# A two-layer decoder step: the odd layer's pool latents kept on chip, its recurrence cut in quarters, and query weights requested earlier

## The reference, cut to what matters

```
u, cq, ckv, kpe = split(rms_norm(x) @ w_in)              # 512 + 256 + 128 + 32 columns
# C: diagonal complex state space, 32 groups x 64 states, in and out 512 channels
s_t = abar * s_{t-1} + bbar u_t ;  y = Re(C s) + D u ;  z = gelu(y);  oc = z * sigmoid(z w_glu + b)
# D: latent attention, 8 heads; prompt: causal over 256 tokens
q = (rms_norm(cq) w_uq), split 64 | 32, normed, second part rotated
# sample: per request 8 pages x 128 cached latents c_all (128 wide) and rotary keys k_all (32 wide)
k = rms_norm(c_all w_uk) * g ;  v = c_all w_uv
o = softmax((q_nope . k + q_pe . k_all) / sqrt(96)) v
x = x + concat(oc, o) @ w_out ;  x = x + peer(rms_norm(x))
```

## Time and profile before

| | |
|---|---|
| median of three executions | 2640.33 us |
| the profiled execution: time, span | 2625.28 us, 2623.6 us |
| PE busy | 2120.1 us, 81% of the span |
| DVE busy | 1206.9 us, 46% |
| ACT busy | 630.0 us, 24% |
| POOL busy | 956.5 us, 36% |
| mean DMA rate | 202 GB/s |
| mean granted TensorE clock | 0.89 |

### The profile page before, as it was taken

The page is one execution under the profiler, slowest core; times in us unless marked ns, Lnnn a source line. Parts: engine busy times, 40 slices in busy tenths (PEclk is TensorE's granted clock), DMA queues, the critical chain, the costliest instruction groups (busy, mean ns, idle before and its releaser), DMA issues.

```text
span 2623.6 us, 36788 instructions
## 1 busy us (share of the span) xinstructions
PE 2120.1 (81%) x13673; PEld 1535.1 (59%) x13673; DVE 1206.9 (46%) x3473; ACT 630.0 (24%) x952; POOL 956.5 (36%) x872
## 2 busy tenths in 40 slices
PE   8897799999998666666667875899999997666665
PEld 3553479999996333333443323489999995333232
DVE  2432369813333533674266453289623333333332
ACT  1421114455552000000133330015455550000000
POOL 0001007970003666666012222018850005656664
PEclk9678899999998888888867887899999998888887
DMA  5415324444447999999400033404445448999998
GB/s 209 171 52 193 114 112 145 154 164 165 166 164 244 356 354 339 338 342 356 153 8 27 27 97 123 152 35 168 153 163 167 163 167 293 353 335 356 355 345 297
DMA packets 163476, 529.55 MB, mean 202 GB/s; under 512 B 20930, under 2 KB 35298, under 8 KB 162786
## 3 DMA queue, kind: packets, MB, share of 16 engines
q0 software_dynamic: 89152, 313.05, 33.0%
q1 hardware_dynamic: 74146, 214.14, 23.7%
HBM read 524.42 MB, written 2.69 MB: 201 GB/s over the span
## 4 chain that ended last, share of the span: by engine, by line
PE 58%; DMA 18%; POOL 10%; issue 7%; DVE 4%; ACT 2%; POOLq 1%; SPq 0%; DVEq 0%; ACTq 0%
DMA v_slot<-in_peer_v,v_rows 16%; PE bank L617 15%; PE bank L762 9%; PE bank L764 9%; PE bank L763 9%; PE bank L821 7%; POOL v_slot L562 6%; POOL u_low L551 3%; PE bank L1050 2%; POOLq L376 1%; PE bank L816 1%; PE bank L637 1%; DMA region<-in_cache_a_kt 1%; PE bank L1056 1%; PE bank L721 1%
## 5 line engine op out<-in xcount | busy, mean ns | idle before, releaser
L562 POOL DMA_INDIRECT v_slot<-in_peer_v,v_rows x576 | 546.1, 948 | 767.9 <-PE bank L764 441.1
L762 PE MATMUL bank<-h_parts,u_high 128*128 128x288 f32 x2048 | 606.6, 296 | 5.1 <-POOL u_low L551 4.6
L763 PE MATMUL bank<-h_parts,u_high 128*128 128x288 f32 x2048 | 604.4, 295 | 0.0
L764 PE MATMUL bank<-h_parts,u_low 128*128 128x288 f32 x2048 | 602.8, 294 | 0.0
L821 PE MATMUL bank<-v_slot,weight_columns 128*32 128x512 f32 x2048 | 321.5, 755 | 273.4 <-DMA v_slot<-in_peer_v,v_rows 269.4
L551 POOL TENSOR_TENSOR u_low<-u_slot,u_high 128x1024 fp32r<-128x1024 f32 x120 | 320.2, 2678 | 369.7 <-ACT u_high L1217 369.6
L762 PEld LDWEIGHTS bank<-h_parts,u_high 128*128 128x128 f32 x2048 | 384.1, 188 | 8.3 <-POOL u_low L551 7.7
L764 PEld LDWEIGHTS bank<-h_parts,u_low 128*128 128x128 f32 x2048 | 385.7, 188 | 0.0
L763 PEld LDWEIGHTS bank<-h_parts,u_high 128*128 128x128 f32 x2048 | 384.5, 188 | 0.0
L1217 ACT CAST u_high<-u_slot 128x1024 fp32r<-128x1024 f32 x256 | 268.8, 1050 | 398.1 <-PE bank L764 287.2
L821 PEld LDWEIGHTS bank<-v_slot,weight_columns 128*32 128x32 f32 x2048 | 72.0, 124 | 395.0 <-issue 343.0
(11 more groups left out here) (337 smaller groups left out, 2140.8 us busy)
## 6 DMA issues: line engine op xcount, KB each, us to landing
u_slot<-in_peer_ut SPq DMA_DIRECT2D x256, 512.0 KB, 3.3
w_q<-in_peer_w_q SPq DMA_DIRECT2D x8, 2048.0 KB, 15.8
v_slot<-in_peer_v,v_rows POOLq DMA_INDIRECT x576, 6.2
region<-in_ev_w_in SPq DMA_DIRECT2D x4, 2048.0 KB, 15.7
region<-in_cache_a_kt SPq DMA_DIRECT2D x8, 960.0 KB, 12.1
region<-in_cache_a_v SPq DMA_DIRECT2D x8, 960.0 KB, 14.3
ckv_pages<-in_pool_ckv SPq DMA_DIRECT2D x52, 128.0 KB, 2.1
region<-in_pool_kv POOLq DMA_DIRECT2D x32, 128.0 KB, 3.1
```

What stands on the lines that cost most here:

```text
L562: pool.indirect_dma_start(out=VS[n % NVS], out_offset=None, in_=v_rows, in_offset=bass.IndirectOffsetOnAxis(ap=IDX[:, t:t + 1], axis=0)).t ...
L762: pe.matmul(bank, uh, HR[:, 0, c, :], start=(c == 0), stop=False)
L763: pe.matmul(bank, uh, HR[:, 1, c, :], start=False, stop=False)
L764: ins = pe.matmul(bank, ul, HR[:, 0, c, :], start=False, stop=(c == KC - 1))
```

## The change

- **Latents on chip.** The turned latents of a request's four pages go to a place of their own (`CKPT`, sixteen tiles, and `CKPT_FIRST`, four, for the first pass) and are read twice, by the key norms and by the scores. The values (the other 64 KB of each page) are fetched apart (`CKPV`). Fetching is split between SP (requests 0, 1, 4, 5) and POOL (2, 3, 6, 7). The first pass is loaded by POOL behind the last expert group of layer 0. No refill waits for squares any more.
- **Recurrence by quarters.** Four quarters of four chunks. The sample states are computed once for all sixteen chunks in a tile of their own (`BUS`) rather than twice for eight.
- **First quarter of the key norms, and quarters 0 and 1 of B u, ahead of the prompt attention.** B is turned at the start of the layer, and the sums' weights `SUMW` are set there.
- **New order.** Key norms, states' outputs, sample scores and values are interleaved; the sample attention for r = 0 runs before the recurrence ends, and the gate before the last values.
- **Early query weights.** The first quarter of `w_q` is requested in layer 0 right behind `w_out`, in layer 1 when the gate and the first values are done. In layer 1 the quarters change places (`W_QS`).

Cut to its core, by engine:

```diff
 SP
+    load(W_QS[0][0], peer_w_q[0, :, :, 0:512])          # behind load(W_OUT, ...)
-    wait states_ready 2; stores of states; 24 full pages; wait y_ready 4; 24 full pages;
-    wait pages_used 1; 4 pages; wait pages_used 4, 6: w_out1 halves
+    wait qct_ready 10;     for b in 0,1: 8 latent pages each;  TBLDN
+    for c in 0,1: wait quarter_ready c+1;  for b in 4,5: 4 latent pages each
+    wait y_ready 2;        for b in 0,1: 8 value pages each
+    wait sd_scores 1;      for b in 4,5: 8 kpe pages each;  for b in 4,5: 8 value pages each
+    wait samples_ready, quarter_ready 4: w_out1 halves;  stores of states
+    wait oc_ready 4, pages_used 4:  load(W_QS[1][0], peer_w_q[1, :, :, 0:512])
 POOL
-    wait qk_ready 3: 32 kpe pages;  wait s5_bt_ready: 64 latent pages, refills wait key_squares
-    then 8 full pages, 32 kpe pages, 4 full pages
+    wait v_used (all of layer 0):  for b in 0..3: first 4 latent pages each
+    wait qct_ready 10:  for b in 2,3: 8 latent pages each;  for b in 0..3: 8 kpe pages each
+    for c in 0,1: wait quarter_ready c+1;  for b in 6,7: 4 latent pages each
+    wait sd_scores 1:   for b in 2,3: 8 value pages each;  for b in 6,7: 8 kpe pages each
+    wait y_ready 4:     for b in 6,7: 8 value pages each
 PE  (odd)
+    turn B;  norm;  w_in1;  latents;  q, k, v of the new tokens
+    states_in(0); states_in(1); B u of the sample rows; key_norms(0,0)
     turn q and k; prompt attention; turn its output
+    states_in(2); absorbed queries
+    key_norms(0,1); states_out(0); states_in(3); key_norms(1,0); states_out(1)
+    sample_states_out(); latent_scores(0); key_norms(1,1); latent_turn(0)
+    states_out(2); latent_values(0); states_out(3); latent_out_turn(0)
+    latent_scores(1); [zg_ready] gate product; latent_turn(1); latent_values(1); latent_out_turn(1)
 ACT (odd), from the copies of q, k, v on
+    qk_root(0); states_in(0); qk_root(1); states_in(1); BUS copies
+    key_squares 0..7; qk_root(2); key_squares 8..15; copies of turned q, k; prompt exps; states_in(2)
+    key_squares 16..31; states_in(3); 32..39; key_root(0); 40..55; latent_exp(0); 56..63
+    latent_turn(0); key_root(1); gelu; latent_exp(1); sigmoid; latent_turn(1)
 DVE (odd), from the per-head norms on
+    key_vars(0,0); QG, QPE copies; prompt attention
+    states_turn/scan/turn_back(0); absorbed_queries; turn/scan/turn_back(1)
+    key_vars(0,1); out_of_states(0); sample_states; states_turn(2); key_vars(1,0)
+    out_of_states(1); out_of_sample_states; states_scan(2); key_scales(0); latent_scores(0)
+    states_turn_back(2); states_turn(3); key_vars(1,1); states_scan(3); out_of_states(2)
+    states_turn_back(3); latent_out(0); out_of_states(3); latent_out_turned(0)
+    key_scales(1); latent_scores(1); gate products; latent_out(1); latent_out_turned(1)
```

More of the change, by code:

```diff
@@ new lines, in build @@
+        states.at += 4096
+        STMP = states.take("s5_sample_tmp", 4, SCH, DEC_B)
+        KPEN = states.take("kpe_new", NS, parts=DR)
+        TBLDN = states.take("mask_new", 2, NS)
+        RKN = states.take("key_scale_new", DH, DEC_T)
+        RKNX = states.take("key_scale_new_x", NS)
+        mid = Row(R2_0 + 3264, R2_0 + 15552)
+        kt0 = mid.at
+        Q = mid.take("mla_q", 3, DH, DQK)
+        KCAT = mid.take("mla_k", 2, DH, DQK)
+        KR = mid.take("mla_k_raw", 3, 512)
+        S_SD = tile_at("mla_sample_scores", [PAST + NS], kt0 + 4 * PAGES * P)
@@ L333, in build @@
         BT = end.take("s5_b_t", 2, 4, P)
-        STMP = end.take("s5_sample_tmp", 4, SG2, DEC_B)
+        end.at += 256
         LASTP = end.take("s5_last_prompt", 2, SCH)
@@ L1012, in odd, with states_in @@
                         pe.matmul(bank[0:rows, :], CKT[:, a:a + rows], w, start=True, stop=True).then_inc(a_full, 1)
+                pe.wait_ge(sem("s5_bt_ready"), 2)
+                def states_in(g):
+                    for s in range(4 * g, 4 * g + 4):
+                        rows = slice(32 * (s % 4), 32 * (s % 4) + 32)
+                        for k in range(2):
+                            bank = to_act()
+                            pe.matmul(bank[:, 0:SEQ], BT[rows, k, g, :], UT[rows, g, 0:SEQ], start=True, stop=True).then_inc(a_full, 1)
@@ new lines, in odd @@
+                states_in(0)
+                states_in(1)
+                four = [to_act() for _ in range(4)]
+                for g in range(4):
+                    for k in range(2):
+                        for q in range(4):
+                            rows = slice(32 * q, 32 * q + 32)
+                            ins = pe.matmul(four[q][:, (4 * k + g) * NS:(4 * k + g) * NS + NS], BT[rows, k, g, :], UT[rows, g, SEQ:NT], start=True, stop=True)
+                            if g == 3 and k == 1:
+                                ins.then_inc(a_full, 1)
@@ L1315, in odd, with states_in, qk_root @@
                         act.activation(ST8I[0:rows, m, 0:3], ST8[0:rows, m, 0:3], ACT.Sqrt).then_inc(sem("latent_rinv"), 1)
+                def states_in(g):
+                    for q in range(4):
+                        for k in range(2):
+                            copy_out(BU[g][:, k, q, :], full()[:, 0:SEQ], "bu_ready")
+                def qk_root(t):
+                    rows = TILES[t][1]
+                    act.wait_ge(sem("qk_var"), t + 1)
+                    act.activation(ST8I[0:rows, t, 0:24], ST8[0:rows, t, 0:24], ACT.Sqrt).then_inc(sem("qk_rinv"), 1)
                 for t, rows, a in TILES:
@@ L1370, in odd @@
                         act.nop().then_inc(sem("sd_pt"), 1)
+                key_squares(16)
+                key_squares(24)
+                states_in(3)
+                key_squares(32)
+                key_root(0)
+                key_squares(40)
+                key_squares(48)
+                latent_exp(0)
+                key_squares(56)
+                latent_turn(0)
+                key_root(1)
+                act.wait_ge(sem("y_ready"), 5)
+                for m in range(4):
+                    act.activation(ZG[:, m, :], Y[:, m, :], ACT.Gelu_apprx_tanh).then_inc(sem("zg_ready"), 1)
+                latent_exp(1)
+                for m in range(4):
+                    bank = full()
+                    link(act.activation(SGM[:, m, :], bank[:, 0:NT], ACT.Sigmoid, bias=BGLU[:, m:m + 1]))
+                    act.nop().then_inc(a_free, 1)
+                    act.nop().then_inc(sem("sgm_ready"), 1)
+                latent_turn(1)
                 act.wait_ge(sem("qabs_ready"), 1)
@@ L2013, in odd, with key_scales, out_of_states @@
-                dve.wait_ge(sem("key_roots"), 1)
-                link(dve.reciprocal(RK, RK))
-                for r in range(2):
+                    say("samples_ready")
+                def key_scales(r):
+                    dve.wait_ge(sem("key_roots"), r + 1)
+                    link(dve.reciprocal(RK[:, r, :], RK[:, r, :]))
+                def out_of_states(g):
+                    bank = full()
+                    STT(Y[:, g, 0:SEQ], UT[:, g, 0:SEQ], DSKIP[:, g:g + 1], bank[:, 0:SEQ], ALU.mult, ALU.add)
+                    free()
+                    say("y_ready")
```

498 lines of the change are left out of this document (288 added, 210 removed).

## The result

The changed kernel takes 2570.05 us (median of 4 runs, 2563.28 to 2577.24) beside 2642.72 us for the kernel before (4 runs): a ratio of **0.9729, 95% interval 0.9689 to 0.9769**. The prediction was 2565 us with a range of 2545 to 2600, and faster. Timed once more in a later comparison it gave 0.9716 (0.9679 to 0.9754), 2550.08 beside 2625.13: 72.7 and 75.1 us less, where 75 were forecast.

What follows compares the result with a forecast made beforehand. No engine is full: in the odd mixer's attention and the 251 us behind it, engines take turns, and PE waited 45 us for latent pages. Mixer 65 plus query weights 10 gives 75 us off 2640.3: 2565, range 2545 to 2600.

Steps and rivals of the forecast that it cites:

- The sum: Whole kernel: 65 us less in the odd mixer plus 10 from early query weights, 75 us in all, predicted median 2565.
- the query weights: Before the first query product in both layers: waits of 5.4 and 5.2 us, 0.2 kept each, so 10.2 us go.
- Part 1: Odd mixer, ahead of the prompt attention: work moved there makes the attention end 23.2 us later.
- The third root: First key-norm pass: root of the third tile comes 8 us late, but DVE still ends at 1364, under the pass.
- interference of the first loads: POOL's latents beside `w_in1` and small inputs: between 0 and 3.5 us, 2.5 taken as cost.
- Part 2: Odd mixer, behind the prompt attention: engine-by-engine layout to output projection at 1572.2; 1574.7 with 2.5 us of load interference, against 1639.5.
- The rule of the table loads: ACT in mid-pass: skill's 1.38 us drain per table load would end two passes 1.4 us later, gain 72; rows followed instead.
- 1 (the order catches, 45): Mixer passes and scores each wait 6 to 8 us more than laid out; 30 us go, gain 45, 2595; chance 0.17.
- 2 (better, 92): Attention at full clock saves 4 us, no load interference 2.5, passes closed up 10; gain 92, 2548; chance 0.10.
- 3 (POOL held by DVE): Each of POOL's 104 path loads waits 1.22 us for DVE's product; 45 us slower, 2685; chance 0.04.
- 4: Gains eaten to within 13 us, as by loads arriving late at several passes at once; 2635; chance 0.03.
- The small slacks: Page loads behind the attention: all land just in time, with 0.6 to 4.6 us in hand.

## Why the prediction was right

**The sum.** Forecast 64.8 for the mixer, measured 62.9. Forecast 10.2 for the query weights, measured 4.6 + 6.0, and 10.6 by undoing them. 75.0 against 73.5, and 72.7 and 75.1 by the medians. Agreement to 2 us is partly luck, as steps below are off by up to 2.5 us each, in both directions.

**Part 1.** The first score operation stood 86.3 us behind the first product of `w_in1` (1358.42 in the earlier trace rows; 1272.17) and stands at 113.1, and at 110.3 to 113.1 in the variants that leave this part alone: 24 to 27 us later, where 23.2 and 2.5 of interference were forecast. The pass took 25.3 us, not 24.1, and the sample rows' B u with its copies 5.0, not 3 (1349.27 to 1354.24). The third root was late (DVE waited 11.55 us for it) and hidden, as said. Against these stands the interference of the first loads: the new tokens' values end at 60.8 to 63.2 us of the mixer with the loads in the way and at 61.3 with them later (61.6 before), so it cost up to 1.6 us in the profiled execution and nothing in others, in place of 2.5.

**Part 2.** From the first score operation to the output projection it was 281.1 us; forecast 190.6, measured 191.3. The steps: quarters 20.2 (20.0), passes 25.2 to 26.3 (24.1 to 25.6), sample states 13.0 (11.5), absorbed queries 3.6 (2.0), sample outputs 0.9 (2), quarter output 1.1 (1.2), values 8.8 (10.6), reciprocal 6.55 (6.5). The errors are of both signs and cancel: what DVE's sample states took more, the values gave back. Sixteen of their products now take 1.91 us where the earlier trace rows had 3.62, at a granted clock of 1.00 (1567 to 1572) and behind the gate product; before, PE had just waited 3.92 us for the exponent and the clock was 0.50 (1623 to 1627). The sum had carried the slower price over. The waits came where they were laid out: DVE for the last sums 7.29 (7.2), PE for score banks 10.36 and 3.13. The wait of 45.3 us for pages is gone. It was worth 34.7 us of path by the run that took it out alone, and 26.8 of the mixer in that kernel's own order; the 33 us behind the last sums came with the new order, by the timelines.

**What it did not see.** The sum priced the four parts of the title as one layout and said of the first pass only that it is gone from behind. It never set the 24 us at the head against what DVE would wait without it. The run that moves it back shows them equal. The forecast was right because the layout was right, not because each part pays.

**The rule of the table loads.** ACT's timeline in the last pass, table load, exponent and the next square:

```profile
1516.94 1.28 ACT L1452 ACT_TABLE_LOAD   x1 [0.17 <-ACT key_squared L1427]
1518.23 1.18 ACT L1452 ACTIVATE mla_sample_scores<-mla_sample_scores,region 128x1056 f32<-128x1056 f32 x1
...
1519.41 0.58 ACT L1427 ACTIVATE key_squared<-bank 128x512 f32<-128x512 f32 x1
```

The exponent starts 0.01 us behind the 1.28 of the load, the load 0.17 behind the square. The Trainium skill, "ScalarE: Activation LUTs", section "What ACT_TABLE_LOAD costs", has a drain of about 1.38 us on top of each load; none shows in these rows. The time of the whole kernel can't decide it: the gain came out at 72.7 and 75.1 in two comparisons, and 72 and 75 are within the spread.

**Rivals.** 1 (the order catches, 45): the catches were there, but no larger than laid out, 13.5 us in the score banks. 2 (better, 92): the attention again ran at about half the clock, 0.51 over its 32 us, though entered from a full pass at 0.97; its length did not change. 3 (POOL held by DVE): 95 of the 110 intervals between like loads in the mixer are between 1.10 and 1.20 us, beside DVE's products too; the last eight loads follow by about 1.27, also where DVE stands idle. The Trainium skill, "SBUF — State Buffer", section "SBUF: two separate sides", has descriptor writing for POOL's DMAs blocked while DVE runs an operation in a two-port mode, and has a DVE operation with two SBUF inputs block only GpSimd operations that read SBUF. The products here have two SBUF inputs, and the trace agrees: beside them the loads keep their 1.15 us. 4 fell with the result. The small slacks, though, were the right thing to name: 2.6 us were given for the last values, and when DVE got 10.4 us faster, that load became the bound at once.

## What to carry to other kernels

When a wait of one engine is taken away, lay out the others to the next waits before choosing the order: here work moved ahead of the attention cost on one side just what it saved on the other, and only an order that filled DVE's waits brought more (5.4 us in one pair of profiles). Small loads on a queue are a resource with a length of their own (96 at 1.15 us on two queues): write their finish beside each engine's, and share them before shortening an engine that is level with them. Read a change of 1% by the stages of the profile, not by the span: a stage full of transfers that the change does not touch moved by 16 us from one execution to another.

## What the runs showed of the hardware

- The gather of value rows, DMA busy at 0.92 to 0.94, took 433 to 453 us for the same instructions; the windows over it show 343 GB/s where it took 437 and 330 where it took 453. It is the largest difference between these profiles of like kernels.
- A 64 KB load issued 5 us behind a 2 MB one was used 5.2 us after its issue by a PE that waited for it, and 3.3 us after when the big one was held back. Behind 4 MB of output weights such loads took 5.3 us to land (median of 17).
- The prompt attention had a granted clock of 0.51 over its 32 us, about the lower of the two levels, although the 28 us straight ahead of it (PE busy for 21.8) had 0.97; without that pass ahead it had 0.50.
- A load of 64 KB with its address from a register follows the one before by 1.15 us on POOL (median) and by 1.10 on SP.
- The same sixteen records of value products took 1.91 us at a granted clock of 1.00 and 3.59 to 3.62 at 0.50; each time at 0.50, PE had waited 3.9 us or more shortly before.
